# RWKV scan: the state scaled by the chunk's decay on ScalarE instead of GpSimd, under new order tables

## The chip, the cores and the metric

The kernel runs on one NeuronCore of a Trainium2 chip. The metric is the device time of one execution in microseconds; the median of several executions counts. TensorE is called PE here, VectorE DVE, ScalarE ACT and GpSimd POOL, as the profile does.

## What is computed

The reference is one inference step of a two-layer trunk with 640 tokens (512 latent, 128 context). Layer 0 mixes by attention and a gated linear recurrence, layer 1 by a bidirectional RWKV-7 scan, and each is followed by an MLP. The change touches the scan of layer 1 alone. Per head (16 heads of 64 channels) and per direction the reference runs

```
def step(s, inp):
    r_t, w_t, k_t, v_t, kk_t, a_t = inp
    sa = einsum('bhvk,bhk->bhv', s, -kk_t)
    s = s * w_t[:, :, None, :] + sa[..., None] * (kk_t * a_t)[:, :, None, :] + v_t[..., None] * k_t[:, :, None, :]
    return s, einsum('bhvk,bhk->bhv', s, r_t)
```

over the tokens, forwards and backwards. The kernel does it in chunks of 64 tokens: inside a chunk all is written as matrix products, and only the state `s`, 64x64 per head, passes from chunk to chunk. What comes out of a chunk is, by channel, decay times old state plus decay times the chunk's increment, where decay is the product of `w` over the chunk.

## The kernel before

The scan takes two heads at a time (a pair `q`, 0 to 7) and walks a pair in 5 tiles of 128 tokens, two chunks each, forwards and backwards at once. That gives 40 iterations `n`, and 5 of them make a pair. Below, turn 0 to turn 4 is the iteration with `n % 5` equal to 0 to 4.

Every engine has one queue of instructions that it runs strictly in order. What stands in it is laid out in Python: `run_iteration` goes through a table of names (`PE_ORDER`, `PE_FIRST`, `DVE_ORDER`, `ACT_FIRST`, `ACT_ORDER`, `POOL_ORDER`) and calls for each entry the task of that name, for iteration `n` plus the number beside the name. The engines meet by semaphores that each task waits on and raises. Nothing else sets the order. The tasks that matter here:

- **G, A1, A2, A3** prepare a chunk's inverse two or three iterations ahead: PE multiplies, DVE or ACT takes the product out of PSUM, POOL adds the identity (L2615 in `start`, L2622 in `plus_one`), and PE multiplies again.
- **GR, B1 to B5, BT** prepare the rest of the next iteration. For GR, DVE masks two 128x512 blocks (L2499).
- **x, u, s** are the walk itself, once for each of two chunks (x0, u0, s0, then x1, u1, s1; s1 stands in the next iteration). x: PE reads the state, DVE adds (L2520). u: PE multiplies that, ACT evacuates it (L2404). s: PE forms the increment, DVE writes the new state (L2531) from the increment and from `S2`, the old state times the decay.
- **S2** is made by POOL in its task x (`s2`, L2607): one 128x128 multiply of two state slices with a broadcast decay. It waits for the old state; DVE's `walk_s` waits for it.
- **y**: ACT evacuates the outputs of the iteration before (L2413). PE's x0 waits for it.
- **Once per pair**, for this pair or the next: the projections `prompt`, `w`, `a` with sigmoids on ACT (L2323, L2325), `cum0`, `cum1` (DVE scan L2446 and subtraction L2447), `keys0` to `keys3` (DVE, L2456 to L2470), `decays` (ACT), `staging` (DVE, four instructions L2476 to L2479 a tile), `k_sum`, `bonus_raw` (DVE, L2567 and L2568), `bonus`, `values`, `y_sum` (DVE L2552), `mean`, `var`, `y_norm` (L2560, L2561, L2564), `gate` (L2544), `final`, `state`.

DVE's entry for s, on which the change bears most, is in the code

```
dve.wait_ge(S("rwkv_s_psum"), k + 1)
dve.wait_ge(S("rwkv_s2"), k + 1)
```

and then one scalar_tensor_tensor for each direction.

Of the kernel before, what the change touches and what calls it, by code (L numbers as in the profile page):

```python
# [115 lines left out]
def program(nc, a, o):  # L116
    with ExitStack() as ctx:
# [1881 lines left out]
        def place(q, c):  # L1999
# [13 lines left out]
        DVE_ORDER = ("k_sum", "values", ("G", 2), "mean", "B5", ("s1", -1), ("keys2", -1), ("GR", 1), ("keys0", 1), "y_sum", "x0", "staging3", ("cum0", -1), "cum1",
                     "staging4", "staging1", "y_norm0", "keys3", "staging2", "s0", ("B3", 1), "staging0", ("bonus_raw", -1), "x1", "y_norm1", ("A3",
                     2), "keys1", ("B4", 1), ("gate", 1))
        ACT_FIRST = (("decays0", -1), ("decays3", 2), ("y1", -1), ("bonus", -1), ("mean", -1), ("a", -1), ("k_square", 2), ("state", 2), ("B1", 1), ("A1", 2), "decays1",
                     ("decays4", 2), "prompt", "u0", ("A2", 2), "var", ("final", -1), ("k_sum", 2), ("B2", 1), "w", ("BT", 1), "u1", ("decays2", 2))
# [284 lines left out]
        def rwkv_act(act, step):  # L2302
# [103 lines left out]

            def walk_y(n, s):
# [10 lines left out]
            tasks.update(dict(u=walk_u, y=walk_y, ahead=lambda m: out_ahead_act(act, m)))  # L2418
# [174 lines left out]
        def rwkv_pool(pool, step):  # L2593
# [428 lines left out]
```

## Time and profile before

| | us |
|---|---|
| median of three executions | 2197.14 (2193.59 to 2198.74) |
| the profiled execution | 2194.96 |
| its span, first to last instruction | 2193.2 |
| the scan within it | about 1187 to 1705 |
| a pair of the scan in the middle | 61.48 |

Of the page, the first part gives for each engine the busy time over the whole span: PE 93%, DVE 64%, ACT 47%, POOL 14%. This is an average over stages with different limits. Outside the scan PE multiplies large blocks nearly without a pause, and nothing there is touched. Inside the scan PE, DVE and ACT pass small blocks to one another. The profile is read there by turn: busy time of each engine in each of the five turns of one pair, then the pauses of PE and what ended them, then the single instructions around those pauses.

### The profile page before, as it was taken

Reading aid. Unit: us, or ns where it says so; the run is one execution under the profiler, and the core shown is the slowest. Engines: PE = TensorE matmul, PEld = TensorE weight load, DVE = VectorE, ACT = ScalarE, POOL = GpSimd, SP = SyncE. Lnnn points to the kernel's source line nnn. Section 1 sums busy time; section 2 is a strip of 40 time slices with the busy share of each in tenths; the row PEclk is TensorE's granted clock in tenths of the full one; section 3 lists DMA queues with packets and bytes.
Section 4 is the critical chain, followed back from the end, with each engine's and each line's share of the span. In section 5 each row is a group of like instructions: output and inputs, shape, how many; then the busy total and the mean of one; then the engine's idle time right before and its main releaser. Section 6 shows DMA issues by size and latency. Waiting matters only on the chain.

```text
span 2193.2 us, 60459 instructions
## 1 busy us (share of the span) xinstructions
PE 2041.7 (93%) x26203; PEld 1834.8 (84%) x26203; DVE 1408.8 (64%) x2698; ACT 1040.2 (47%) x1887; POOL 310.2 (14%) x542
## 2 busy tenths in 40 slices
PE   5999877898999999989998899999989999999999
PEld 3689754478999999967997777777777999999999
DVE  2242375655666666777644888888885478585757
ACT  5252354443535353567333666666664264434353
POOL 1000131001000000010001544444442200000000
PEclk8999999999999999999998999999999999999999
DMA  8212205960131313113210000000000211222312
GB/s 284 86 39 80 80 1 204 371 241 20 59 115 58 97 58 97 59 40 124 78 42 8 8 7 10 8 11 10 10 26 25 97 58 62 93 80 75 97 58 87
DMA packets 129764, 167.86 MB, mean 77 GB/s; under 512 B 13900, under 2 KB 87388, under 8 KB 129372
## 3 DMA queue, kind: packets, MB, share of 16 engines
q1 hardware_dynamic: 129500, 164.00, 22.3%
q8 instruction: 208, 3.41, 0.6%
q14 instruction: 56, 0.46, 0.1%
HBM read 160.44 MB, written 3.54 MB: 75 GB/s over the span
## 4 chain that ended last, share of the span: by engine, by line
PE 76%; DVE 9%; issue 7%; ACT 4%; POOL 2%; DMA 1%; PEld 1%; PEldq 0%; POOLq 0%; DVEq 0%; SPq 0%; ACTq 0%
PE psum L178 74%; ACT arena L1857 1%; DVE arena L2499 1%; ACT arena L1411 1%; DVE arena L2446 1%; PEld psum L178 1%; DMA arena<-in_x_prompt 1%; DVE small L1377 1%; PE psum L1342 0%; DVE arena L2470 0%; PE psum L2242 0%; POOL arena L2615 0%; ACT arena L642 0%; POOL arena L621 0%; DMA arena<-in_ada_w 0%
## 5 line engine op out<-in xcount | busy, mean ns | idle before, releaser
L178 PE MATMUL psum<-arena 64*64 64x64 f32 (+5 forms) x16064 | 575.2, 239 | 88.4 <-DVE arena L2520 16.4
L178 PEld LDWEIGHTS psum<-arena 64*64 64x64 f32 (+3 forms) x16064 | 460.2, 140 | 219.4 <-issue 102.7
L178 PE MATMUL psum<-hidden_high,weights_high 128*128 128x320 f32 x896 | 277.1, 309 | 0.5 <-DVE arena L1020 0.5
L178 PE MATMUL psum<-hidden_high,weights_low 128*128 128x320 f32 x896 | 276.9, 309 | 0.0
L178 PE MATMUL psum<-hidden_low,weights_high 128*128 128x320 f32 x896 | 276.9, 309 | 0.0
L178 PE MATMUL psum<-norm_low,weights_high 128*128 128x320 f32 x960 | 218.8, 309 | 0.0
L178 PE MATMUL psum<-norm_high,weights_low 128*128 128x320 f32 x960 | 218.7, 309 | 0.0
L178 PE MATMUL psum<-norm_high,weights_high 128*128 128x320 f32 x960 | 218.7, 309 | 0.0
L178 PEld LDWEIGHTS psum<-hidden_high,weights_high 128*128 128x128 f32 x896 | 168.2, 188 | 0.9 <-issue 0.7
L178 PEld LDWEIGHTS psum<-hidden_low,weights_high 128*128 128x128 f32 x896 | 168.2, 188 | 0.0
L178 PEld LDWEIGHTS psum<-hidden_high,weights_low 128*128 128x128 f32 x896 | 168.2, 188 | 0.0
L178 PEld LDWEIGHTS psum<-norm_high,weights_low 128*128 128x128 f32 x960 | 160.6, 188 | 0.0
L178 PEld LDWEIGHTS psum<-norm_high,weights_high 128*128 128x128 f32 x960 | 160.5, 188 | 0.0
L178 PEld LDWEIGHTS psum<-norm_low,weights_high 128*128 128x128 f32 x960 | 160.5, 188 | 0.0
L999 DVE TENSOR_TENSOR hidden<-hidden 128x640 f32<-128x640 f32 x32 | 26.4, 825 | 176.3 <-ACT hidden L946 176.3
L944 ACT ACTIVATE hidden<-psum 128x640 f32<-128x640 f32 x64 | 45.1, 705 | 189.7 <-PE psum L178 189.7
L899 ACT ACTIVATE weights_high<-weight_sums 128x512 fp32r<-128x512 f32 x128 | 76.8, 624 | 106.6 <-DVE weight_sums L918 55.6
L621 POOL TENSOR_TENSOR arena<-arena 128x640 f32<-128x640 f32 x24 | 41.7, 1738 | 569.8 <-ACT arena L613 569.1
L1020 DVE SCALAR_TENSOR_TENSOR arena<-psum,ada,arena 128x128 f32<-128x128 f32 (+2 forms) x208 | 83.4, 429 | 30.1 <-PE psum L178 29.2
L903 DVE TENSOR_TENSOR weights_low<-weight_sums,weights_high 128x512 fp32r<-128x512 f32 x128 | 88.1, 699 | 8.4 <-ACT weights_high L899 8.4
L899 ACT ACTIVATE weights_high<-weights 128x512 fp32r<-128x512 f32 x96 | 58.2, 622 | 68.3 <-PE psum L178 68.3
L2615 POOL TENSOR_TENSOR arena<-arena,constants 64x128 f32<-64x128 f32 x160 | 66.5, 415 | 157.3 <-DVE arena L2490 144.3
(268 smaller groups left out, 3986.7 us busy)
## 6 DMA issues: line engine op xcount, KB each, us to landing
weights<-in_mlp_w SPq DMA_DIRECT2D x64, 1024.0 KB, 5.3
arena<-in_ada_w SPq DMA_DIRECT2D x24, 2048.0 KB, 9.3
arena<-in_ab_w_in SPq DMA_DIRECT2D x6, 2048.0 KB, 7.8
arena<-in_ab_w_out SPq DMA_DIRECT2D x2, 2048.0 KB, 8.6
arena<-in_rwkv_wv SPq DMA_DIRECT2D x2, 2048.0 KB, 7.9
arena<-in_rwkv_wr SPq DMA_DIRECT2D x2, 2048.0 KB, 8.1
arena<-in_rwkv_wk SPq DMA_DIRECT2D x2, 2048.0 KB, 8.1
arena<-in_x_sample SPq DMA_DIRECT2D x1, 2048.0 KB, 10.0
```

The source lines that it names most:

```text
L178: return nc.tensor.matmul(out, lhsT, rhs, start=start, stop=stop, skip_group_check=shared)
L621: G.tensor_tensor(total, a0 if k == 1 else total, (a0, a1)[k % 2], ALU.add).then_inc(S("norm_squares_added"), 1)
L899: A.activation(slots_of(WHI)[:, j], slot_raw(l, grp, i, j), ACT.Copy).then_inc(S("slot_high"), 1)
L903: V.tensor_tensor(slots_of(WLO)[:, j], slot_raw(l, grp, i, j), slots_of(WHI)[:, j], ALU.subtract)\
L944: A.activation(h, PS[:, 2 * j:2 * j + 2, 0:HN], ACT.Relu).then_inc(S("up_evacuated"), 1)
L999: V.tensor_tensor(h[:, H_T1:H_T3 + 1, :], h[:, H_B11:H_B22 + 1:3, :], h[:, H_B12:H_B12 + 1, :].broadcast_to([P, 2, HN]), ALU.subtract)\
L1020: ins = V.scalar_tensor_tensor(x, PS[:, bank, c:c + t1 - t0], gate[:, m, g:g + 1], x, ALU.mult, ALU.add)
L1377: step(V.tensor_reduce(st[:, 0:1], pair(2 * h, k), AXX, ALU.max))
L1411: A.activation(PR[m % 2][:, h, 0:k], pair(2 * h, k), ACT.Exp, scale=ATTN_SCALE, bias=st[:, 1:2], accum_out=st[:, 2:3]).then_inc(S("att_exp ...
L1857: A.activation(XI[s % 2][:, k, :], unit(U_H, 8)[:, k, :], ACT.Identity, scale=OMM[:, 8 * mrow + k:8 * mrow + k + 1])\
L2446: step(V.tensor_tensor_scan(y, m, x, 0.0, ALU.mult, ALU.add))
L2615: ins = G.tensor_tensor(P1[HALF[h], d, 0], QD[r, h, 0], units(r), ALU.add)
```

## The change

POOL's task for S2 goes. ACT gets a task `decayed_state` under the name x: two ACTIVATE copies of 128x64, one for each direction, from the state to `S2`, each with the decay column as its per-partition scale. It waits for the same two semaphores, and raises the same one, which DVE's `walk_s` still waits on. All order tables are written anew. PE's, DVE's and POOL's work is otherwise the same, instruction for instruction.

```
+            def decayed_state(n, s):
+                (cs, us), k = steps_of(n, s), 2 * n + s
+                act.wait_ge(S("rwkv_state"), k)
+                act.wait_ge(S("rwkv_state_in"), n // 5 + 1)
+                for d in range(2):
+                    ins = A.activation(S2[:, d, :], ST[d][:, cs[d], :], ACT.Copy, scale=PE_[:, (n // 5) % 2, d, cs[d]:cs[d] + 1])
+                ins.then_inc(S("rwkv_s2"), 1)
...
-            def s2(n, s):
-                (cs, us), k = steps_of(n, s), 2 * n + s
-                pool.wait_ge(S("rwkv_state"), k)
-                pool.wait_ge(S("rwkv_state_in"), n // 5 + 1)
...
-                G.tensor_tensor(S2, st, dec.broadcast_to([P, 2, 64]), ALU.mult).then_inc(S("rwkv_s2"), 1)
-                pool.wait_ge(S("rwkv_s2"), 2 * n + s + 1)
...
-        POOL_ORDER = ("G", ("B0", -1), ("x0", -2), "A1", "A2", ("x1", -2))
+        POOL_ORDER = (("A2", -2), ("G", -1), ("B0", -2), ("A1", -1))
```

What the tables move, as it stands in the queues, turn by turn:

| turn | before | after |
|---|---|---|
| 0, DVE | GR, keys0, y_sum, x0 | GR, y_sum, x0 |
| 0, PE | GR, B1, A1, prompt, x0, u0, B2, A2, w | GR, A1, x0, B1, prompt, u0, A2, B2, w |
| 0 to 4, ACT | y1, (decays), B1, A1, ... u1 | y1, S2 of x0, A1, B1, (decays), ... S2 of x1, u1 |
| 1 to 4, PE | GR, B1, x0, A1, ... u0 | GR, A1, B1, x0, ... u0 |
| 1, DVE | x0, cum0, cum1, s0, B3, x1, A3, keys1, B4 | x0, keys0, cum0, cum1, s0, B3, keys1, x1, A3, B4 |
| 1 and 2, PE | var of the pair before stands behind the G that ends turn 1 | var stands before u1 of turn 1 |
| 2, DVE | B5, s1, keys2, GR, x0, y_norm0, keys3 | B5, y_norm0, s1, GR, x0, keys2, keys3 |
| 2 and 3, PE | gate, u1, G, B5, final, s1 | final, u1, gate, G, B5, s1 |
| 3 and 4, DVE | bonus_raw before x1 of turn 4 | bonus_raw before x1 of turn 3 |

On DVE, turn 1 of pair 3 (iteration 16), before: the new state of turn 0 (L2531), the masks of GR (L2499), x0 (L2520), the two cumulations, s0 and what follows.

```order
L2531 SCALAR_TENSOR_TENSOR arena<-psum,arena 128x64 [waits rwkv_s2,rwkv_s_psum]
...
L2499 TENSOR_TENSOR arena<-psum,constants 128x512 [waits rwkv_s_psum,b_product]
...
L2520 TENSOR_TENSOR arena<-psum,arena 128x128 [waits b_scalar,rwkv_x_psum]
L2446 SCALAR_TENSOR_TENSOR arena<-constants,arena 128x640 [waits rwkv_sig]
L2447 TENSOR_TENSOR arena<-arena 128x640 [waits vector_step]
L2446 SCALAR_TENSOR_TENSOR arena<-constants,arena 128x640 [waits rwkv_sig]
L2447 TENSOR_TENSOR arena<-arena 128x640 [waits vector_step]
L2531 SCALAR_TENSOR_TENSOR arena<-psum,arena 128x64 [waits rwkv_s2,rwkv_s_psum]
...
L2510 TENSOR_TENSOR arena<-psum,arena 128x256 [waits b_product]
L2520 TENSOR_TENSOR arena<-psum,arena 128x128 [waits b_scalar,rwkv_x_psum]
L2505 TENSOR_TENSOR arena<-psum,constants 128x256 [waits a_product]
```

The same place of the changed kernel, whose line numbers are 9 higher here:

```order
L2540 SCALAR_TENSOR_TENSOR arena<-psum,arena 128x64 [waits rwkv_s2,rwkv_s_psum]
...
L2508 TENSOR_TENSOR arena<-psum,constants 128x512 [waits rwkv_s_psum,b_product]
...
L2529 TENSOR_TENSOR arena<-psum,arena 128x128 [waits b_scalar,rwkv_x_psum]
L2465 TENSOR_SCALAR small<-param_cols 128x1
L2469 SCALAR_TENSOR_TENSOR arena<-arena,param_cols 128x640 [waits rwkv_staged,rwkv_k_rs,vector_step]
L2455 SCALAR_TENSOR_TENSOR arena<-constants,arena 128x640 [waits rwkv_sig,vector_step]
L2456 TENSOR_TENSOR arena<-arena 128x640 [waits vector_step]
L2455 SCALAR_TENSOR_TENSOR arena<-constants,arena 128x640 [waits rwkv_sig]
L2456 TENSOR_TENSOR arena<-arena 128x640 [waits vector_step]
L2540 SCALAR_TENSOR_TENSOR arena<-psum,arena 128x64 [waits rwkv_s2,rwkv_s_psum]
```

The two instructions of keys0 (L2465, L2469) now stand between x0 and the cumulations, so ahead of s0.

On ACT, turn 0 of pair 3 (iteration 15), before: y1 (L2413), B1 (L2384), A1 (L2376), the table load and the sigmoids of `prompt`, and u0 (L2404).

```order
L2413 ACTIVATE arena<-psum 128x128 [waits rwkv_ysum,rwkv_state]
...
L2384 ACTIVATE arena<-psum 128x512 [waits b_product]
L2376 ACTIVATE arena<-psum 128x512 [waits a_product]
L2323 ACT_TABLE_LOAD [waits rwkv_lora,rwkv_staged]
L2323 ACTIVATE arena<-psum,param_cols 128x128 [waits rwkv_bonus_raw]
...
L2404 ACTIVATE arena<-psum 64x128 [waits rwkv_u_psum]
...
L2380 ACTIVATE arena<-psum 128x768 [waits a_product]
```

And in the changed kernel, where y1 is L2422, A1 L2377, B1 L2385, u0 L2405 and the copies of S2 are L2413:

```order
L2422 ACTIVATE arena<-psum 128x128 [waits rwkv_ysum,rwkv_state]
...
L2413 ACTIVATE arena<-arena 128x64 [waits rwkv_state_in,rwkv_state]
L2413 ACTIVATE arena<-arena 128x64
L2377 ACTIVATE arena<-psum 128x512 [waits a_product]
L2385 ACTIVATE arena<-psum 128x512 [waits b_product]
L2324 ACT_TABLE_LOAD [waits rwkv_lora,rwkv_staged]
L2324 ACTIVATE arena<-psum,param_cols 128x128 [waits rwkv_bonus_raw]
...
L2405 ACTIVATE arena<-psum 64x128 [waits rwkv_u_psum]
```

The two copies came in ahead of A1 and B1, and A1 and B1 changed places; the table load, the sigmoids and u0 stand as they did.

## Rows read from the trace of the kernel before

**Rows 1.** Page, part 1: busy time, share of the span, instructions.
```profile
PE 2041.7 (93%) x26203; PEld 1834.8 (84%) x26203; DVE 1408.8 (64%) x2698; ACT 1040.2 (47%) x1887; POOL 310.2 (14%) x542
```
**Rows 2.** Windows, turns 0 to 4: length, busy us of PE, PEld, DVE, ACT, POOL; clock.
```profile
1386.03:1399.57 13.54, 11.79 (x407) 9.78 (x400) 8.42 (x21) 9.63 (x22) 5.82 (x12) 1.00 0.01 4
1399.57:1412.18 12.61, 11.55 (x379) 9.34 (x375) 11.58 (x22) 8.78 (x20) 5.84 (x12) 1.00 0.02 6
1412.18:1424.85 12.67, 10.86 (x366) 9.28 (x366) 12.30 (x27) 7.20 (x17) 5.81 (x12) 1.00 0.01 3
1424.85:1436.24 11.39, 11.25 (x396) 9.83 (x390) 10.07 (x25) 6.06 (x16) 5.20 (x12) 1.00 0.08 17
1436.24:1447.51 11.27, 11.00 (x386) 9.56 (x380) 10.23 (x27) 7.56 (x23) 5.51 (x12) 1.00 0.09 22
```
**Rows 3.** Waits of PE in 1285 to 1592 (five pairs): total us, times, longest.
```profile
PE psum L178 <- DVE arena L2520: 9.6, 10, 1.4
PE psum L178 <- DVE arena L2531: 5.4, 10, 0.7
```
**Rows 4.** Timeline, DVE, turn 0: start us, us, engine, line, [idle before <-releaser].
```profile
1388.46 1.29 DVE L2499 TENSOR_TENSOR arena<-psum,constants 128x512 f32<-128x512 f32 x2 [0.36 <-PE psum L178]
...
1389.85 0.94 DVE L2460 SCALAR_TENSOR_TENSOR arena<-arena,param_cols 128x640 f32<-128x640 f32 x1
...
1391.68 0.29 DVE L2520 TENSOR_TENSOR arena<-psum,arena 128x128 f32<-128x128 f32 x1
```
**Rows 5.** Timeline, PE, turn 0.
```profile
1392.02 4.62 PE L178 MATMUL psum<-arena 64*64 64x64 f32 x176 [1.44 <-DVE arena L2520]
...
1393.64 1.09 PE L178 MATMUL psum<-arena 64*64 64x512 f32 x8
```
**Rows 6.** Timeline, ACT, turn 0.
```profile
1390.61 1.28 ACT L2323 ACT_TABLE_LOAD   x1 [0.42 <-PE psum L178]
1391.90 1.14 ACT L2323 ACTIVATE arena<-psum,param_cols 128x128 f32<-128x128 f32 x4
1392.91 0.55 ACT L2404 ACTIVATE arena<-psum 64x128 f32<-64x128 f32 x2
```
**Rows 7.** Timeline, DVE, turn 1.
```profile
1401.99 1.29 DVE L2499 TENSOR_TENSOR arena<-psum,constants 128x512 f32<-128x512 f32 x2 [0.61 <-PE psum L178]
1403.19 0.28 DVE L2520 TENSOR_TENSOR arena<-psum,arena 128x128 f32<-128x128 f32 x1
...
1408.17 0.47 DVE L2531 SCALAR_TENSOR_TENSOR arena<-psum,arena 128x64 f32<-128x64 f32 x2
```
**Rows 8.** Timeline, PE, turn 1.
```profile
1408.69 2.47 PE L178 MATMUL psum<-arena 64*64 64x64 f32 x104 [0.61 <-DVE arena L2531]
```
**Rows 9.** Timeline, DVE, end of turn 2 and turn 3.
```profile
1423.81 0.41 DVE L2506 COPY arena<-psum 128x256 f32<-128x256 f32 x1
...
1427.54 1.29 DVE L2499 TENSOR_TENSOR arena<-psum,constants 128x512 f32<-128x512 f32 x2 [0.61 <-PE psum L178]
```
**Rows 10.** Timeline, PE, end of turn 2 and turn 3.
```profile
1424.37 1.16 PE L178 MATMUL psum<-arena 64*64 64x64 f32 x48 [0.47 <-DVE arena L2506]
1425.34 0.45 PE L178 MATMUL psum<-constants,arena 64*64 64x64 f32 x8
```
**Rows 11.** Lines in 1285 to 1592: xcount, busy us, mean ns, idle before.
```profile
L2371 ACT ACTIVATE arena<-arena 128x256 f32<-128x256 f32 x25 | 10.2, 410 | 0.0
...
L2335 ACT ACTIVATE arena<-psum 128x64 f32<-128x64 f32 x10 | 1.7, 222 | 0.1
```
**Rows 12.** Lines in 1285 to 1592, DVE and POOL.
```profile
L2479 DVE TENSOR_TENSOR arena<-arena 128x256 f32<-128x256 f32 x25 | 14.7, 589 | 0.0
...
L2568 DVE SCALAR_TENSOR_TENSOR arena<-arena,param_cols 128x640 f32<-128x640 f32 x5 | 4.5, 907 | 0.2
...
L2607 POOL TENSOR_TENSOR arena<-arena 128x128 f32<-128x128 f32 x50 | 25.4, 508 | 6.3 <-POOL arena L2622 2.5
```
**Rows 13.** Timeline, POOL, around the cumulations of turn 1.
```profile
1402.91 0.40 POOL L2607 TENSOR_TENSOR arena<-arena 128x128 f32<-128x128 f32 x1
```

More of the change, by code:

```diff
@@ L2001, in place @@
             return c if c < 8 else c + 2 * (q % 2)
-        PE_ORDER = ("prompt", "mean", "var", "B5", ("final", -1), ("s1", -1), ("GR", 1), ("B1", 1), "x0", ("A1", 2), "a", "w", "state", "bonus", "u0", ("B2", 1), ("A2",
-                     2), "s0", ("B3", 1), ("BT", 1), "x1", ("A3", 2), ("B4", 1), ("values", 1), ("k_sum", 1), ("gate", 1), "u1", ("G", 3))
+        PE_ORDER = ("mean", "B5", ("s1", -1), ("GR", 1), ("A1", 2), ("B1", 1), "x0", "state", "a", "bonus", "u0", ("B2", 1), ("A2", 2), "s0", ("B3", 1), "prompt", ("BT",
+                     1), "x1", "w", ("A3", 2), ("B4", 1), ("var", 1), ("values", 1), "final", ("k_sum", 1), "u1", ("gate", 1), ("G", 3))
         def with_ahead(order, after):
@@ L2013, in program @@
[L2013 to L2017, printed above, removed]
+        PE_FIRST = ("B5", ("bonus", 1), ("s1", -1), ("GR", 1), ("A1", 2), "x0", ("B1", 1), "prompt", "u0", ("A2", 2), ("B2", 1), ("mean", -1), "w", ("state", 1), "s0",
+                     ("k_sum", 2), ("A3", 2), ("final", 1), ("B3", 1), "x1", ("a", -1), ("BT", 1), ("B4", 1), "u1", ("G", 3), ("var", -1), ("gate",
+                     2), ("values", 2))
@@ new lines, in program @@
+        DVE_ORDER = ("values", "k_sum", "gate", ("G", 2), "mean", "B5", "y_norm0", ("s1", -1), ("GR", 1), "y_sum", "x0", "staging3", "keys0", "staging1", "staging4",
+                     "staging2", ("cum0", -1), ("keys2", -1), "cum1", "keys3", "s0", ("B3", 1), "bonus_raw", "y_norm1", "keys1", "x1", "staging0",
+                     ("A3", 2), ("B4", 1))
+        ACT_FIRST = (("k_sum", 2), ("decays2", 2), ("decays0", -1), "decays1", ("decays4", 2), ("y1", -1), "x0", ("A1", 2), ("B1", 1), "prompt", ("k_square", 2), ("mean",
+                     -1), "u0", ("A2", 2), ("state", 2), ("B2", 1), ("a", -1), ("bonus", -1), "w", ("BT", 1), "x1", "var", ("decays3", 2), ("final",
+                     1), "u1")
@@ L2019, in first_of_pair @@
         def first_of_pair(n):
             return n >= 0 and n % 5 == 0 and n + 5 < NB
-        ACT_ORDER = (("y1", -1), "decays2", "decays3", ("B1", 1), ("A1", 2), "a", "decays4", "bonus", "u0", "state", ("B2", 1), ("A2", 2), "mean", ("decays1", 1),
-                     ("k_square", 1), ("BT", 1), "prompt", ("decays0", 1), "u1", ("k_sum", 1), "final", "w", ("var", 1))
-        POOL_ORDER = ("G", ("B0", -1), ("x0", -2), "A1", "A2", ("x1", -2))
+        ACT_ORDER = ("decays3", "decays0", "mean", ("y1", -1), "x0", ("A1", 2), ("B1", 1), ("decays1", 1), "decays2", "decays4", "state", "a", "bonus", "u0", ("B2", 1),
+                     ("A2", 2), "w", ("k_square", 1), ("BT", 1), "final", "x1", ("var", 1), "u1", ("k_sum", 1), "prompt")
@@ L2652, in rwkv_pool @@
             tasks = dict(G=start, A1=squares, A2=fourths, B0=values)
-            tasks.update(dict(x=s2))
             for n in range(-4, NB + 2):
```

9 lines of the change are left out of this document (1 added, 8 removed).

## The prediction

> **What bounds the kernel now.** The page comes first: PE is busy 93% of the span [rows 1], but most of that is large products outside the scan, which the change leaves alone. So I read the scan, and there one pair by its five turns [rows 2]. They take 13.54 + 12.61 + 12.67 + 11.39 + 11.27 = 61.48 us. PE is busy 56.45 us of it, DVE 52.60, ACT 39.23, POOL 28.18. The reader is to see two things. PE is nearly full in turns 3 and 4 (11.25 of 11.39, 11.00 of 11.27), and DVE is nearly full in turn 2 (12.30 of 12.67). And the slack lies in turns 0 to 2, where PE stands still for 1.75, 1.06 and 1.81 us. That is 5.03 us a pair with the 0.4 of turns 3 and 4, and no reordering can win more. The granted clock is 1.00 in all five, so the clock plays no part.
>
> The pauses of PE that have a name are waits for DVE's x (L2520, 9.6 us in five pairs) and for the new state (L2531, 5.4 us) [rows 3]. POOL's multiply, which the change removes, is not among them. The chain through the pauses is always the same: PE has run ahead, and DVE still has something in its queue before the entry that PE wants.
>
> **S2 leaves POOL.** Ten multiplies a pair of 508 ns [rows 12] are 5.1 us of POOL's 28.2. POOL is busy under half of a pair, so on the path this is worth nothing directly. What it can free is DVE, which slows down beside POOL: the last instruction of a staging (L2479) takes 589 ns on average [rows 12], where an instruction of DVE on 256 columns alone takes 0.41 us (L2506, [rows 9]). That is 0.18 us for each of five stagings, 0.9 us a pair, most of it in turns 3 and 4, where DVE is not the bound, and some of it beside POOL work that stays. I take 0.2 us a pair over all of DVE's work where it is the bound, and keep 0 and 0.6.
>
> The Trainium skill (SBUF, on the shared port pair) says that a GpSimd instruction and a DVE instruction with two SBUF inputs exclude each other for the whole instruction. By that, DVE would be held off for up to the length of each multiply. What it would give as a result is a rival below.
>
> **S2 comes to ACT.** Two copies of 128x64, ten times a pair. The same shape from PSUM without a scale column takes 222 ns, and ten of them, in twos, are 1.7 us busy; a larger one from SBUF takes 410 ns for 128x256 [rows 11]. So two of them take between 0.34 and 0.82 us, and I take 0.5, nearer to the row of the same shape. ACT gets 5 us a pair more and is then busy 44 of 61.5. The S2 of x1 stands before u1, for which ACT waits anyway. The S2 of x0 stands behind y1 and ahead of A1 and B1. Behind it in ACT's queue are A1, B1 and later u0; A1's evacuation is wanted by POOL and then by the end of A2 on PE, B1's by B2. PE now runs A1 ahead of B1 and x0, so that its product is ready for ACT sooner by what these take, more than the 0.5 of the copies. In turn 2, where y1 comes late, B1 should come out of ACT about when PE reaches B2; I put 0.1 us on this, inside the sum of turns 2 and 3. I cost the S2 of x0 at nothing elsewhere. If that cover were gone it would cost up to 0.5 us in each turn.
>
> **A1 before x0 on PE, turns 1 to 4.** PE's u0 wants DVE's x0, which stands behind the two masks of GR, 1.29 us [rows 7]. While they run PE has the same A1, B1 and x0 to do in either order. The order costs nothing as long as the masks set the time.
>
> **Turn 0: keys0 leaves, and B1 and prompt go between x0 and u0.** Before, DVE runs masks, keys0 (to 1390.79), y_sum, and only then x0, done at 1391.97 [rows 4]; PE starts u0 at 1392.02 after 1.44 us of standing still [rows 5]. Without keys0 x0 is done 1.1 us earlier, about 1390.8. But ACT is next: the table load can't start before PE's prompt is done (1390.61), and load, sigmoids and u0's evacuation run to 1393.46 [rows 6] whether u0 is early or not. PE's w has to wait until the sigmoids of prompt have read its banks, 1391.90 + 1.14 = 1393.04. In the trace PE starts w at 1393.64 [rows 5], so w can move forward by some 0.55 us, no more. s0 and all behind it follow w. **Gain 0.55**, between 0.3 (A3 finds POOL late) and 1.1.
>
> **Turn 1: keys0 arrives.** Between DVE's x0 (done at 1403.47) and the new state (begun at 1408.17) there are only the cumulations, 4.7 us, and PE waits 0.61 us for that state [rows 7, 8]. With keys0 between, which was the time from the masks' end at 1389.75 to 1390.79 [rows 4], this is later by 1.1 us, and PE is already waiting. **Cost 1.1**, between 0.9 and 1.2. Here DVE is the bound and stays it up to the gate of turn 2: B3, keys1, A3, the G masks, y_norm0, keys2 and keys3, staging0. The tables permute these, and DVE runs them without a pause before and after, so their order neither gains nor costs. var before u1 makes the evacuation of u1 on ACT late by about 1 us; DVE has y_norm0 ahead of s1 in that time, which covers it.
>
> **Turns 2 and 3: final moves.** Before, PE gets out of DVE's hold at 1424.37 (G, 0.47 us after it was ready, behind DVE's A3 [rows 9, 10]) and has G, B5, final (0.45 [rows 10]), s1 and GR to do until the masks at 1427.54, for which DVE waits 0.61 us [rows 9]. After, final is done while PE waits for DVE's A3 anyway, with gate behind it. The masks can begin earlier by final and about 0.2 of that pause, at most by the 0.61 that DVE waits. **Gain 0.6**, between 0.3 and 0.6.
>
> **Turns 3 and 4: bonus_raw moves forward by a turn.** Its second instruction takes 0.91 us [rows 12] and its first about as much, both in front of DVE's x1. In turn 3 DVE is idle 11.39 - 10.07 = 1.3 us and in turn 4 1.0 us [rows 2], so of 1.8 us put into turn 3 up to 0.5 stick out, and PE, which was idle for 0.14 us there, follows: **cost 0.3**, between 0 and 0.6. Turn 4 is relieved: **gain 0.15** of PE's 0.27 us of pause.
>
> **The sum.** -0.55 + 1.1 - 0.6 + 0.3 - 0.15 = +0.1, and -0.2 for DVE without the multiplies: -0.1 us a pair. Turns of this kind come seven times (keys0 and cumulations for pairs 1 to 7), so -0.7 us; the first and the last turns of the scan have neither keys nor sigmoids in new places and I put them at 0. The profiled execution of 2194.96 us, 1.8 of it outside its span of 2193.2, becomes 2194.3. The median of the three runs is 2.2 above it, so 2196.4.
>
> **Rivals.** Forecast: as summed, within 0.2% (4.4 us), which is about what a measurement of this kernel can tell from no change. The cases:
>
> 1. Slower, 2202. The 1.1 us of keys0 is the mechanism. It decides if DVE, from x0 of turn 1 to the masks of turn 3, gives nothing back: then final's place saves nothing (PE would then wait for DVE's masks and not DVE for PE), DVE's relief is 0, and +1.1 - 0.55 + 0.3 - 0.15 = +0.7 a pair, times 7 is +4.9; with bonus_raw at its upper bound +7. For it: DVE is busy 12.30 of 12.67 in turn 2. Against: DVE does wait 0.61 us before the masks of turn 3 [rows 9]. 0.26.
> 2. Faster, 2189. The pause before u0 (1.44) goes by 1.1 and not by 0.55, because w finds room elsewhere in PE's queue, and DVE gains 0.6 instead of 0.2: -0.1 - 0.55 - 0.4 = -1.05 a pair, -7.4. For it: 1.44 is the longest pause of the pair. Against: the sigmoid chain on ACT, which has no slack in the rows. 0.20.
> 3. Faster, 2184. POOL's multiplies hold DVE off for their whole length, and their absence sets it free where it is the bound: four multiplies in turns 1 and 2 of 0.40 us are -1.6 a pair, -1.7 with the sum, -12. Against it: a multiply at 1402.91 lies inside the masks of turn 1 [rows 13], and these take 1.29 us there as in turn 0, where no multiply does [rows 4, 7]. By that rule of the Trainium skill (SBUF) only instructions with two SBUF inputs would be held, and the masks read PSUM, so the trace doesn't contradict it. 0.12.
> 4. Slower, 2214. The S2 of x0 is exposed on ACT in each turn: 0.5 x 5 = 2.5 us a pair over 7 pairs, +17.5. For it: ACT is in the walk's chain by u. Against: it is idle 22 us of the pair [rows 2], and 0.42 us right before the table load [rows 6]. 0.04.
>
> **How the numbers follow.** The forecast has 0.38. Same by more than 0.2% in neither direction: 0.38. Faster: 0.20 + 0.12 = 0.32. Slower: 0.26 + 0.04 = 0.30. The range takes in cases 1 to 3 with the bounds of the unknown costs: low ends 0.3 + 0.5 for turn 0 and DVE's relief give -12 over seven pairs, high ends (bonus_raw 0.6, final 0.3, turn 0 0.3, keys0 1.2) give +1.1 a pair, +8, and some exposed S2 on top. I give 2184 to 2208.
>
> **What would show it.** Right: in a middle pair of the changed kernel PE waits for x (L2529) well under 1.44 us in turn 0 and 1.5 to 1.9 us for the state (L2540) in turn 1; the pair takes 61 to 62 us; DVE's idle time before the masks of turn 3 stays at some 0.6 us or less; ACT is busy about 44.5 us a pair. Wrong: a pause of PE before B2 or the end of A2 that ACT ends (case 4), cumulations and key steps on DVE that got visibly shorter (case 3), or a turn 1 that doesn't grow by a microsecond. What would upset the sum is a wait that the trace of before doesn't show at all, since every turn of this scan is held by three queues at once.

## The result, and the profile after it

The changed kernel takes 2204.89 us (median of 6 runs, 2203.32 to 2209.69), the kernel before 2197.15 us (6 runs, 2191.82 to 2198.74): ratio 1.0039, 95% interval 1.0027 to 1.0051. It is slower by 7.7 us. The time lies in the range of 2184 to 2208, but the forecast, no difference that can be measured, was wrong: the change costs. The profiled executions are 2194.96 us before and 2204.85 us after, with spans of 2193.2 and 2203.1 us.

Page of the changed kernel, part 1, against [rows 1]:

```profile
PE 2054.6 (93%) x26203; PEld 1844.0 (84%) x26203; DVE 1405.8 (64%) x2698; ACT 1075.9 (49%) x2047; POOL 265.6 (12%) x462
```

S2 has moved as the change says: POOL has 80 instructions and 45 us less, ACT 160 instructions and 36 us more. But PE is busy 13 us longer for the same 26203 products. Busy time alone doesn't say why: part of it comes at an unchanged clock (57.28 us in a middle pair without a stretch at half clock, 56.45 before). So the granted clock has to be read beside it.

The windows of the changed kernel, against [rows 2]. The first five rows are the turns of the pair that starts at 1329.25, the sixth is turn 1 of the next pair, the last a stretch inside that turn. Columns: length, busy us of PE, PEld, DVE, ACT, POOL with counts, granted clock, DMA share, GB/s.

```profile
1329.25:1342.29 13.04, 12.13 (x403) 9.82 (x396) 7.09 (x19) 10.92 (x27) 4.64 (x10) 1.00 0.03 6
1342.29:1356.00 13.71, 11.42 (x379) 9.47 (x376) 12.57 (x23) 9.07 (x20) 4.53 (x10) 1.00 0.01 2
1356.00:1368.74 12.74, 11.49 (x388) 9.76 (x380) 12.23 (x27) 8.90 (x27) 4.97 (x10) 1.00 0.03 7
1368.74:1380.28 11.54, 11.32 (x388) 9.73 (x381) 10.88 (x27) 6.98 (x20) 4.22 (x10) 1.00 0.05 13
1380.28:1391.46 11.18, 10.91 (x392) 9.58 (x385) 9.41 (x25) 8.03 (x25) 4.24 (x10) 1.00 0.09 22
1404.50:1419.71 15.21, 12.93 (x379) 10.43 (x377) 12.56 (x23) 9.29 (x20) 4.53 (x10) 0.89 0.01 4
1415.90:1419.30 3.40, 3.40 (x45) 2.33 (x44) 2.00 (x6) 1.59 (x2) 0.00 (x0) 0.51 0.00 0
```

The reader is to compare the second row with the sixth. It is the same turn with the same 379 products and the same work of DVE, once 13.71 us at a granted clock of 1.00, once 15.21 us at 0.89. In the second case PE spends 3.4 us at half clock (1.2 of 2.4 GHz), where only 45 products are run, and the turn is 1.50 us longer.

Such stretches of 3.4 us begin in the changed kernel at 1228.1, 1289.6, 1415.9 and 1542.1, always in turn 1 of a pair, in pairs 0, 1, 3 and 5. From the first B5 of the scan on, the seven pairs of the kernel before have none. First the four stretches, then those seven pairs before:

```profile
1228.10:1231.50 3.40, 3.12 (x86) 2.94 (x78) 2.34 (x6) 0.81 (x3) 0.00 (x0) 0.50 0.03 5
1289.60:1293.00 3.40, 3.40 (x49) 2.31 (x42) 2.40 (x6) 1.31 (x2) 0.00 (x0) 0.50 0.00 0
1415.90:1419.30 3.40, 3.40 (x45) 2.33 (x44) 2.00 (x6) 1.59 (x2) 0.00 (x0) 0.51 0.00 0
1542.10:1545.50 3.40, 3.40 (x57) 2.39 (x54) 1.72 (x5) 1.89 (x3) 0.00 (x0) 0.51 0.00 0
```
```profile
1203.70:1634.70 431.00, 391.91 (x13191) 333.44 (x13181) 367.05 (x816) 275.99 (x670) 199.13 (x420) 1.00 0.04 9
```

This is no accident of the profiled executions. The mean granted clock of the whole span is 0.978 to 0.981 in all six executions of the changed kernel, and 0.980 to 0.987, on average 0.984, in the 83 executions of the kernel before that ran beside the experiments. Four stretches of 3.4 us at half clock take 0.003 off the mean.

From the first B5 to the B5 seven pairs later the pairs take, in us:

| pair | 0 | 1 | 2 | 3 | 4 | 5 | 6 | sum |
|---|---|---|---|---|---|---|---|---|
| before | 59.33 | 61.48 | 61.48 | 61.48 | 61.79 | 62.56 | 62.79 | 430.92 |
| after | 60.58 | 63.70 | 62.21 | 63.71 | 62.21 | 64.16 | 63.02 | 439.59 |

The difference is 8.67 us. (The spans differ by 9.9. The other 1.2 us arise ahead of pair 0, 0.9 of it in code that the change leaves alone, and nothing is added behind the seven pairs.) Four stretches at 1.50 us are 6.0 of it, and 2.7 is the order itself: +0.73 in pair 2 (62.21 against 61.48), which would be 2.2 for pairs 1 to 3, and smaller amounts in the others. The 1.50 is measured in pairs 1, 3 and 5, where turn 1 takes 15.2 us and not 13.7; in pair 0 it is taken over from them.

PE's waits in 1285 to 1592 after the change (total us, times, longest), against [rows 3]:

```profile
PE psum L178 <- DVE arena L2540: 9.8, 5, 2.0
PE psum L178 <- ACT arena L2405: 4.4, 14, 0.7
PE psum L178 <- DVE arena L2529: 3.8, 10, 0.4
PE psum L178 <- ACT arena L2324: 2.1, 5, 0.6
```

The long waits have changed their kind. Before, there were ten for x with 9.6 us, at most 1.4. Now five waits for the new state make 9.8 us, 2.0 each: one a pair, in turn 1. This is the place in the pair from 1391.46, first on PE and then on DVE:

```profile
1414.96 1.51 PE L178 MATMUL psum<-arena 64*64 64x64 f32 x56 [1.95 <-DVE arena L2540]
1416.22 2.38 PE L178 MATMUL psum<-arena,constants 64*64 64x320 f32 x8
```
```profile
1408.26 0.29 DVE L2529 TENSOR_TENSOR arena<-psum,arena 128x128 f32<-128x128 f32 x1
1408.65 0.97 DVE L2469 SCALAR_TENSOR_TENSOR arena<-arena,param_cols 128x640 f32<-128x640 f32 x1
1409.66 1.49 DVE L2455 TENSOR_TENSOR_SCAN arena<-constants,arena 128x640 f32<-128x640 f32 x1
...
1414.44 0.46 DVE L2540 SCALAR_TENSOR_TENSOR arena<-psum,arena 128x64 f32<-128x64 f32 x2
```

keys0 (L2469) stands between x0 and the cumulations, and the state comes at 1414.44, 6.2 us after x0 instead of 5.0 [rows 7]. PE stands still for 1.95 us. Then x1, A3 and B4 (56 instructions) take 1.51 us and `var` (64x320, eight instructions) 2.38. In the pair before the pause is 1.96 us, the clock stays at 1.00, and the same instructions behind it take the usual 1.28 and 1.26:

```profile
1352.76 1.28 PE L178 MATMUL psum<-arena 64*64 64x64 f32 x56 [1.96 <-DVE arena L2540]
1353.86 1.26 PE L178 MATMUL psum<-arena,constants 64*64 64x320 f32 x8
```

### The profile page after: what moved, and what is told of

It is laid out like the page before. It is cut to its first block, busy times and chain, and to the rows that moved or that the text cites. A ratio compares the mean times of both kernels' runs of the same rounds, so it can differ in the third digit from the quotient of the medians.

```text
span 2203.1 us, 60533 instructions
## 1 busy us (share of the span) xinstructions
PE 2054.6 (93%) x26203; PEld 1844.0 (84%) x26203; DVE 1405.8 (64%) x2698; ACT 1075.9 (49%) x2047; POOL 265.6 (12%) x462
## 4 chain that ended last, share of the span: by engine, by line
PE 78%; ACT 7%; issue 7%; DVE 6%; DMA 1%; POOL 1%; PEld 1%; PEldq 0%; POOLq 0%; DVEq 0%; ACTq 0%; SPq 0%
PE psum L178 76%; ACT arena L1857 1%; ACT arena L1411 1%; DVE arena L2508 1%; PE psum L2243 1%; PEld psum L178 1%; DVE small L1377 1%; DMA arena<-in_x_prompt 0%; PE psum L1342 0%; ACT arena L642 0%; DMA arena<-in_ada_w 0%; POOL arena L1754 0%; DVE arena L1385 0%; ACT L2324 0%; ACT arena L2405 0%
## 5 line engine op out<-in xcount | busy, mean ns | idle before, releaser
L178 PE MATMUL psum<-arena 64*64 64x64 f32 (+5 forms) x16064 | 584.9, 240 | 87.8 <-ACT arena L1411 14.8
L178 PEld LDWEIGHTS psum<-arena 64*64 64x64 f32 (+3 forms) x16064 | 467.4, 141 | 221.3 <-issue 96.6
```

The costliest lines, as they stand in the source:

```text
L178: return nc.tensor.matmul(out, lhsT, rhs, start=start, stop=stop, skip_group_check=shared)
```

## The experiments

Three theories stood against each other. **T1, order and clock:** keys0 in turn 1 makes the pause, the pause costs 1.1 us by itself, and 1.5 more wherever a stretch at half clock follows. **T2, order alone:** the stretches only come along, and the time is lost in DVE's and ACT's queues. **T3, S2 on ACT:** the copies delay what ACT owes to PE. All ratios are against the kernel before, run on the same chip beside them. The rows come from four chips, so where two rows are compared with each other, their ratios count more than their times.

| run | us | before | ratio (95%) | half-clock stretches | first seven pairs, us |
|---|---|---|---|---|---|
| s2_alone | 2196.96 | 2198.05 | 0.9996 (0.9986 to 1.0007) | 1 | 432.58 |
| tables_alone | 2209.92 | 2198.05 | 1.0049 (1.0037 to 1.0062) | 6 | 448.17 |
| keys0_turn0 | 2192.57 | 2198.05 | 0.9976 (0.9968 to 0.9985) | 0 | 428.69 |
| filled_pause | 2205.29 | 2198.05 | 1.0037 (1.0021 to 1.0052) | 0 | 441.19 |
| filled_wide | 2201.48 | 2197.47 | 1.0020 (1.0011 to 1.0029) | 0 | 437.21 |
| keys0_moved_alone | 2208.43 | 2197.47 | 1.0049 (1.0037 to 1.0062) | 4 | 442.39 |
| cum1_late | 2206.88 | 2197.47 | 1.0044 (1.0032 to 1.0057) | 5 | 443.66 |
| bonus_turn4 | 2189.90 | 2197.47 | 0.9966 (0.9955 to 0.9977) | 0 | 428.91 |
| keys0_turn0_pool | 2196.84 | 2196.76 | 1.0003 (0.9992 to 1.0014) | 1 | 433.39 |
| keys0_behind_x0 | 2192.75 | 2196.76 | 0.9983 (0.9973 to 0.9992) | 0 | 430.02 |
| y_norm0_behind | 2202.73 | 2196.76 | 1.0028 (1.0017 to 1.0038) | 4 | 439.71 |
| var_behind | 2200.48 | 2198.26 | 1.0013 (1.0003 to 1.0023) | 1 | 439.92 |

**s2_alone: the old tables, S2 on ACT.** `decayed_state` with x0 behind y1 and x1 before u1 on ACT, all other order as before.

> The kernel before with its own order tables; only S2 moved from GpSimd to ScalarE (copies for x0 right behind y1, for x1 right ahead of u1). Theory P (the pause of turn 1: keys0 ahead of the cumulations costs 1.1 us a pair and lets the clock fall): no long pause is made here, so about 2197 (2193 to 2200), pair 61.3 to 61.6, clock 1.00 through the scan. Rival S (the two copies on ScalarE, 0.58 us each time, hold up the evacuations): 2201 to 2205, with waits of PE for ScalarE grown.

No difference that can be measured, and one stretch at half clock, in turn 0 of pair 5, where none was expected. So T3 falls: the copies are not what costs.

**tables_alone: the new tables, S2 on POOL.** `decayed_state` out, `s2` back on POOL at its old place:

```
-        ACT_ORDER = ("decays3", "decays0", "mean", ("y1", -1), "x0", ("A1", 2), ...
+        ACT_ORDER = ("decays3", "decays0", "mean", ("y1", -1), ("A1", 2), ...
-        POOL_ORDER = (("A2", -2), ("G", -1), ("B0", -2), ("A1", -1))
+        POOL_ORDER = ("G", ("B0", -1), ("x0", -2), "A1", "A2", ("x1", -2))
```

> The new order tables of PE, DVE and ScalarE with S2 still on GpSimd, in GpSimd's old order. Theory P: like the changed kernel, 2203 to 2207, pause of PE before x1 of turn 1 about 1.9 us, pair 62.2, or 63.7 with a stretch at half clock. Rival S: 2195 to 2199, since ScalarE does no S2.

The tables alone cost 11 to 12 us (by the ratio and by the medians), with six stretches and an undisturbed turn 1 of 13.9 us. So the loss is in the tables. By its first seven pairs, 448.17 us against 439.59, S2 on ACT would even give something back under the new tables, though some 3 us of that are the two stretches more; the intervals of the two ratios overlap, so this run doesn't settle it.

**keys0_turn0: the changed kernel with keys0 back in turn 0**, though behind x0, not in front of it:

```
-... ("GR", 1), "y_sum", "x0", "staging3", "keys0", "staging1", ...
+... ("GR", 1), "y_sum", "x0", ("keys0", 1), "staging3", "staging1", ...
```

> The changed kernel with keys0 taken from turn 1 back to turn 0, but behind DVE's x0, where DVE stood idle for 3.4 us in the kernel before. Theory P: turn 1 shrinks from 13.7 to 12.6 us, turn 0 stays at 13.0, no stretch at half clock inside the pairs, pair 61.1: 2205 - 7 x 1.1 - 4 x 1.5 = 2191 (2188 to 2195). Rival S: not below 2199. Rival O (the other moved entries, var, bonus_raw, A1 before x0, are what costs): 2197 to 2200.

2192.57 us: 12.3 us less than the changed kernel (14 by the ratios), 5.5 less than before, no stretch at half clock. Turn 0 keeps its gain (13.05 us) and turn 1 falls to 12.59, where the kernel before had 12.61. The waits of PE in the same five pairs as above:

```profile
PE psum L178 <- ACT arena L2405: 5.0, 15, 0.5
PE psum L178 <- DVE arena L2540: 4.2, 5, 0.8
```

One entry of DVE's table makes the whole loss. What it does not tell is how much of that is the pause and how much the clock, since both go together.

**filled_pause and filled_wide: the pause filled.** The changed kernel with products whose result nobody reads, in front of x1 of turn 1. They stand right where the pause was, and the semaphore that they wait for is raised before it. A pair gets eight products of 128 columns in the first kernel (16 instructions) and two of 448 in the second (four instructions):

```
+                if s == 1 and n % 5 == 1 and n < 35:
+                    pe.wait_ge(S("a_scalar"), 2 * (n + 2) + A_SC["Q4"])
+                    for _ in range(2):
+                        mm(PS[:, 0, 64:512], ident, CON[:, 0:448])
```

> The changed kernel with 8 extra 128x128 products with 128 columns, whose result nobody reads, on PE in the pause before x1 of turn 1; they wait only for an evacuation that is long done by then. If the four stretches at clock 0.5 follow from PE standing still, they go, every middle pair takes 62.2 us, and the time is 2205 - 6 = 2199 (2197 to 2201). If the stretches come from elsewhere they stay and the time is 2204 to 2207. If the products stick out of the pause, turn 1 grows.

The stretches are gone, and the time is not: 2205.29 us. For T1 that looked like a refutation. But turn 1 itself takes 13.7 us in each of the pairs 1 to 6, as the undisturbed one of the changed kernel does. The time is lost in other turns: in pair 2, turn 3 takes 13.30 us and not 11.54. The waits of PE between 1200 and 1680 show what stands there; here "issue" stands for time in which PE waits for nothing that the profile shows. First filled_pause, then the changed kernel:

```profile
PE psum L178 <- issue: 12.6, 23, 1.6
```
```profile
PE psum L178 <- issue: 3.4, 11, 0.7
```

This kernel has 9.2 us more of such waits, in 23 places and not 11, over half of them in the first three pairs. None of the other kernels here has more than 6.3 us of them. So the filling most likely spoilt its own test, and I made it out of fewer and wider products.

> The changed kernel with the pause before x1 of turn 1 filled by 2 wide products (128x128 by 448 columns, result unread) instead of the 8 narrow ones, which removed every stretch at half clock but cost 9 us of TensorE's own issue waits. With 4 instructions a pair instead of 16 the issue waits should stay near the 3.4 us of the changed kernel. If the stretches at half clock cost 1.5 us each, this gives 2205 - 6 = 2199 (2197 to 2202), clock 1.00 through the scan, all middle pairs 62.2. If the stretches are not what makes the difference between 62.2 and 63.7: 2204 to 2206.

The place in filled_wide. The 1.95 us of pause are 0.26, and what stands behind them runs at full clock:

```profile
1412.31 1.77 PE L178 MATMUL psum<-constants 128*128 128x448 f32 x4
1414.33 1.28 PE L178 MATMUL psum<-arena 64*64 64x64 f32 x56 [0.26 <-DVE arena L2544]
```

The pair is 62.20 us, against 62.21 undisturbed and 63.71 with a stretch in the changed kernel (first row filled_wide, then the changed kernel):

```profile
1390.83:1453.03 62.20, 59.04 (x1905) 49.06 (x1898) 52.16 (x118) 43.90 (x117) 22.66 (x50) 1.00 0.04 10
```
```profile
1391.46:1455.17 63.71, 58.87 (x1901) 49.27 (x1894) 52.19 (x118) 43.91 (x117) 22.58 (x50) 0.97 0.04 10
```

PE still doesn't get the state any earlier, but the pair costs 1.51 us less. Turn 1 takes 13.69 to 13.78 us in pairs 1 to 6; in the changed kernel it takes 13.7 in three of them and 15.2 in the other three:

```profile
1278.23:1292.01 13.78, 13.25 (x383) 10.22 (x381) 12.51 (x23) 9.07 (x20) 4.54 (x10) 1.00 0.01 4
1403.87:1417.57 13.70, 13.11 (x383) 10.15 (x380) 12.56 (x23) 9.07 (x20) 4.52 (x10) 1.00 0.02 4
1528.27:1541.96 13.69, 13.11 (x382) 10.14 (x380) 12.55 (x23) 9.06 (x20) 4.52 (x10) 1.00 0.01 4
```

The ratio is 1.0020 where the changed kernel has 1.0039; the intervals overlap only at their ends. The difference is 4 us of the 6 that the stretches should be worth. The rest is not accounted for: pairs 1 and 2 take 62.9 and 62.8 us, and the waits for issue, 5.9 us here, are no more than other kernels have without a filling. T2 falls in this form: part of the loss is the clock. The rest, 1.0020, is the order with what the filling itself costs.

**keys0_moved_alone: the kernel before with keys0 alone moved** from turn 0 to behind x0 in turn 1.

```
-... ("GR", 1), ("keys0", 1), "y_sum", "x0", "staging3", ("cum0", -1), ...
+... ("GR", 1), "y_sum", "x0", "keys0", "staging3", ("cum0", -1), ...
```

> The kernel before with one entry moved: DVE's keys0 from turn 0 (ahead of x0) to turn 1 (between x0 and the cumulations), S2 on GpSimd. Theory P: the pause before x1 of turn 1 grows from 0.61 to 1.7 us, turn 1 from 12.6 to 13.7, turn 0 shrinks by up to 0.5 but no more (ScalarE's sigmoids hold w): +0.6 x 7 = +4, and with the stretches at half clock +1.5 each, up to +14: 2201 to 2212. Rival O (the other moves of the tables matter more): 2197 to 2199.

The old tables with this one entry give the pause, the stretches and the time, 1.0049. The turn 1 from 1338.61, without a stretch, takes 14.03 us, with one up to 15.3:

```profile
1349.15 2.48 PE L178 MATMUL psum<-arena 64*64 64x64 f32 x104 [2.04 <-DVE arena L2531]
```

**cum1_late: another way out**, with keys0 in turn 0 and, beside it, cum1 and keys1 moved to the end of turn 1, behind A3 and B4.

> Made from the kernel with keys0 back in turn 0 behind x0 (2192.6): cum1 of turn 1 moved from ahead of s0 to behind A3, and keys1 to behind B4. If the pause of 0.8 us before x1 of turn 1 is DVE's queue alone, it goes, and turn 1 falls from 12.6 to about 11.8: 2192.6 - 7 x 0.8 = 2187. If DVE's work is the bound over turns 1 and 2 as a whole, the pause comes back in turn 2 (before s1 or x0) and the time stays at 2192 to 2193.

A miss. Turn 1 falls only to 12.84, and turn 2 grows to 14.0 without and 14.9 with a stretch. At its start PE waits twice:

```profile
1353.05 3.56 PE L178 MATMUL psum<-arena 64*64 64x64 f32 x112 [0.99 <-DVE arena L2519]
1358.34 0.34 PE L178 MATMUL psum<-arena 64*64 64x64 f32 x8 [1.73 <-ACT arena L2422]
```

cum1 now stands in front of B4, and keys1 in front of B5 and y_norm0 of turn 2. They delay B5, and over the new state that DVE makes behind them also y1 on ACT, for which PE waits next. The 2.4 us of a cumulation cost no less at the end of turn 1 than in front of the state. The run also shows that the stretches are no matter of turn 1 or of keys0: they went to the place where the pause now is.

**bonus_turn4: keys0_turn0, and bonus_raw back before x1 of turn 4** (`"bonus_raw"` becomes `("bonus_raw", -1)`).

> Made from the kernel with keys0 back in turn 0 (2192.6): bonus_raw back from turn 3 to turn 4, where it stood in the kernel before. By the term of the prediction (cost 0.3 in turn 3, gain 0.15 in turn 4) turn 3 falls from 11.54 to about 11.2 and turn 4 grows from 11.18 to 11.3: 2192.6 - 1 = 2191.5. If bonus_raw's place is worth nothing: 2192.6.

Turn 3 is 11.13 us instead of 11.54, turn 4 between 11.41 and 12.05 instead of 11.18. So the entry costs 0.41 us where it is put, and about as much comes back where it is taken away; the first seven pairs take 428.91 us, as in keys0_turn0. At 0.9966 it is the fastest kernel of this study, faster than both, but its interval overlaps that of keys0_turn0, so I claim nothing for this entry.

**keys0_turn0_pool: keys0_turn0 with S2 back on POOL.**

> The new tables with keys0 in turn 0 behind x0 (which gave 2192.6 with S2 on ScalarE), but S2 on GpSimd again. It measures what moving S2 is worth where no stretch at half clock confuses the comparison. By the prediction's term (DVE relieved by 0.2 us a pair, bounds 0 and 0.6): 2192.6 + 1.4, up to + 4.2. By the two kernels with the new tables (turn 1 13.71 against 13.88, turn 2 12.74 against 12.92, pauses counted): 2192.6 + 7 x 0.36 = 2195. If the long pauses of the kernel with the tables alone are needed for its loss: 2192.6.

No different from the kernel before, and 4.3 us slower than keys0_turn0 (5.9 by the ratios), with ratios that lie apart. Under the new tables S2 on ACT is worth something that it isn't under the old ones. In the profiled executions the first seven pairs differ by 4.7 us, of which 2.0 are in pair 0, with its stretch, and 2.7 in pairs 1 to 6. One wait that goes with it, in turn 0, is for POOL. In 1285 to 1592, first here, then in keys0_turn0:

```profile
PE psum L178 <- POOL arena L2623: 3.6, 5, 0.8
```
```profile
PE psum L178 <- POOL arena L2620: 1.6, 5, 0.3
```

The line is POOL's step of A, for which PE waits within A2. In turn 0 the new order of PE has A2 ahead of B2 and so asks for it earlier, and on POOL the multiply of S2 (L2608) stands in front of it; PE waits 0.81 us in the turn from 1323.72, and 0.33 in the same turn of keys0_turn0:

```profile
1328.73 0.98 POOL L2608 TENSOR_TENSOR arena<-arena 128x128 f32<-128x128 f32 x1
1329.79 0.64 POOL L2623 TENSOR_TENSOR arena<-arena,constants 128x256 f32<-128x256 f32 x1
```

The other part is DVE's. In pair 2, turn 0 takes 13.30 us against 13.05 in keys0_turn0, turn 1 12.83 against 12.59 and turn 2 12.94 against 12.75, and in turns 1 and 2 DVE is busy longer by about that, 11.76 against 11.52 and 12.42 against 12.24. The place in turn 1 is keys1, two instructions on DVE with two inputs from SBUF. With a multiply of S2 beside them they take 1.76 us, and in keys0_turn0 1.55:

```profile
1346.54 0.40 POOL L2608 TENSOR_TENSOR arena<-arena 128x128 f32<-128x128 f32 x1
```
```profile
1346.60 1.76 DVE L2465 SCALAR_TENSOR_TENSOR arena<-arena 128x640 f32<-128x640 f32 x2
```
```profile
1346.30 1.55 DVE L2473 SCALAR_TENSOR_TENSOR arena<-arena 128x640 f32<-128x640 f32 x2
```

In this kernel a stretch at half clock also follows a wait for POOL, in pair 0:

```profile
1220.71 2.53 PE L178 MATMUL psum<-arena 64*64 64x64 f32 x44 [1.60 <-POOL arena L2623]
```

**keys0_behind_x0: the kernel before with keys0 moved behind x0**, still in turn 0.

```
-... ("GR", 1), ("keys0", 1), "y_sum", "x0", "staging3", ...
+... ("GR", 1), "y_sum", "x0", ("keys0", 1), "staging3", ...
```

> The kernel before with one entry moved: DVE's keys0 in turn 0 from ahead of y_sum and x0 to behind x0. The pause of PE before u0 (1.44 us) should shrink to about 0.4. By the prediction's reading w is held by ScalarE's sigmoids, so turn 0 falls by 0.5 only, from 13.54 to 13.05: 2197.3 - 3.5 = 2193.8. If ScalarE doesn't hold it, turn 0 falls by 1.1 and the time is 2189.6.

As expected. Turn 0 is 13.08 us in place of 13.54, and the pause of 1.44 us before u0 [rows 5] is 0.47:

```profile
1330.85 5.12 PE L178 MATMUL psum<-arena 64*64 64x64 f32 x176 [0.47 <-DVE arena L2520]
```

All that the change wins in turn 0 comes from keys0 not standing before x0. For that it needn't leave the turn.

**y_norm0_behind: bonus_turn4 with y_norm0 behind x0 of turn 2**, to take away DVE's delay of the masks of GR there.

> Made from the fastest kernel so far (keys0 in turn 0, bonus_raw in turn 4, 2189.9): y_norm0 of turn 2 moved from ahead of s1 to behind x0. PE's pauses of 0.34 to 0.40 us before s1, x0 and u0 of turn 2 should go. If DVE's queue is the bound to the end of turn 2, the time is given back at G there (wait for L2515), and it stays at 2189 to 2190. If not, up to 0.7 us in each of 7 pairs: 2185.

A miss. Turn 2 takes 14.28 us without and up to 15.60 with a stretch. y_norm0 now stands with keys2 and keys3 between x0 and the state, which is later by it, and PE has one long pause there:

```profile
1359.42 1.40 PE L178 MATMUL psum<-arena 64*64 64x64 f32 x56 [2.12 <-DVE arena L2540]
```

**var_behind: bonus_turn4 with var back behind G** on PE, and behind u1 on ACT, so that DVE's masks of G at the start of turn 2, which wait 0.57 us for PE, come sooner.

```
-        PE_ORDER = ("mean", "B5", ...  ("B4", 1), ("var", 1), ("values", 1), "final", ...
+        PE_ORDER = ("mean", "var", "B5", ...  ("B4", 1), ("values", 1), "final", ...
```

> Made from the fastest kernel so far (2189.9): var back behind the G that ends turn 1 on PE, and behind u1 on ScalarE, as in the kernel before. DVE waited 0.57 us for that G at the start of turn 2, which the prediction left out when it called DVE's queue free of pauses there. If that wait is what turns 1 and 2 lost, they shrink together by up to 0.5 us a pair: 2186.5 to 2188. If PE then waits for var's evacuation before GR, as it did by 0.42 us in the kernel before, and DVE's y_norm0 for the same, it is given back: 2190 or more.

A miss too: turns 1 and 2 take 13.67 and 13.09 us in place of 12.58 and 12.74. `var` was what PE ran while DVE did keys1 ahead of x1; without it PE waits for x1 (L2529), and G is not earlier. The row is from pair 5, where a stretch at half clock follows; the wait is 0.72 us in the other pairs too.

```profile
1538.68 1.88 PE L178 MATMUL psum<-arena 64*64 64x64 f32 x48 [0.72 <-DVE arena L2529]
```

## Why the prediction was wrong

**Turn 0, gain 0.55: right.** 13.54 to 13.04, so 0.50. The limit was where the prediction put it: before w PE waits 0.38 us for the sigmoids of ACT (L2324 in the waits above, 2.1 us in five pairs), and before u0 only 0.39 for x.

**Turn 1, cost 1.1: right.** 12.61 to 13.71 undisturbed. The pause is 1.95 us, a little over the 1.5 to 1.9 that were named.

**"DVE runs them without a pause before and after": wrong.** DVE waits 0.57 us at the start of turn 2:

```profile
1356.27 0.69 DVE L2499 TENSOR_TENSOR arena<-psum,constants 128x512 f32<-128x512 f32 x1 [0.57 <-PE psum L178]
```

In the kernel before these masks of G start without a wait. The late state is not the reason: keys0_turn0, where the state comes in time, has the same wait of 0.57 us there. It comes with the other entries, since now x1 stands behind keys1 on DVE, and var (1.26 us) stands ahead of u1 and G on PE. Turn 2 takes 12.74 us instead of 12.67, although DVE has no more to do in it. var_behind shows that the place of var alone is not to blame: without it there the turns are longer.

**Final's move, gain 0.6: mis-sized.** Turn 2 gains nothing (+0.07). Turn 3 without bonus_raw (bonus_turn4) takes 11.13 us where it took 11.39, so 0.26 is what is left of it. **bonus_raw, cost 0.3 and gain 0.15:** 0.41 in turn 3 (11.54 against 11.13); turn 4 goes from 11.27 to 11.18. Turns 2 to 4 together give +0.07 + 0.15 - 0.09 = +0.13, where the sum had -0.6 + 0.3 - 0.15 = -0.45.

**S2 off POOL, relief of DVE 0.2: right in size, not in what becomes of it.** DVE is busy 52.17 us in the pair in place of 52.60, 0.43 less. The staging lines fell from 589, 494, 456 and 450 ns to these, in the same window as [rows 12]:

```profile
L2487 DVE TENSOR_TENSOR arena<-arena 128x256 f32<-128x256 f32 x25 | 14.8, 591 | 0.0
L2486 DVE TENSOR_TENSOR arena<-arena 128x256 f32<-128x256 f32 x25 | 11.3, 454 | 0.0
L2485 DVE TENSOR_TENSOR arena<-arena 128x256 f32<-128x256 f32 x25 | 10.3, 414 | 0.0
L2488 DVE TENSOR_TENSOR arena<-arena 128x256 f32<-128x256 f32 x25 | 10.3, 413 | 0.0
```

A line of 591 ns is still there without any multiply on POOL, now the third and not the last, so the 589 of [rows 12] were not the multiply's doing alone. The four fall from 49.6 to 46.7 us in five pairs, 0.6 us a pair; with S2 alone moved (s2_alone) their mean times sum to 1879 ns instead of 1989. Most of the stagings lie in turns 3 and 4, where DVE is not the bound. Where it is, the relief does shorten a turn: turn 2 of s2_alone takes 12.41 us instead of 12.67, with DVE busy 12.04 instead of 12.30. Turn 4 gives it back (11.61 to 12.21 us in pairs 1 to 5, 11.27 to 11.91 before), for a reason that no run here shows. Rival 3, DVE held off for the length of each multiply and 12 us won, falls: s2_alone takes just the multiplies away and is at 0.9996. The Trainium skill (SBUF — State Buffer, section "SBUF: two separate sides") makes the shared pair of ports an exclusive lock between a GpSimd instruction that reads SBUF and a DVE instruction with two SBUF inputs or in a two-port mode, not between all instructions. The trace agrees with that in kind, since the stagings got faster and the masks from PSUM (L2508, 685 ns on average, 686 before) did not, and since keys1 took 0.21 us longer beside a multiply of 0.40. How much of the ten multiplies lay beside such work was not counted, so the length of the lock stays untested.

**S2 on ACT: 0.5 us for two, off the path: right within its bounds.** 345 ns each, 0.59 for two:

```profile
L2413 ACT ACTIVATE arena<-arena 128x64 f32<-128x64 f32 x96 | 28.0, 345 | 6.5 <-DVE arena L2540 6.5
```

ACT is busy 43.91 us a pair, 44 was named. PE waits 4.4 us for u (L2405) in five pairs, where it was 1.1 before; tables_alone, without the copies, has 3.5 of it, so most of that is the order. Rival 4 falls. What the prediction didn't see is the gain on the other side: with the new order of PE, POOL's step of A would have been late (3.6 us of waits in five pairs of keys0_turn0_pool, 1.6 in keys0_turn0). With the relief of DVE in turns 1 and 2 (0.43 us in pair 2) moving S2 was worth 4.3 us there.

**The sum.** A pair at full clock got +0.73 us. That is the +0.7 of rival 1, and in the main for its reason: keys0's 1.1 us were not given back, and final's place saved nothing in turn 2. Over the scan it makes 2.7 us and not 4.9, because pairs 0 and 4 to 6 lose less than the middle one (pair 4 +0.42, pair 6 +0.23, pair 0 without its stretch -0.25). That rival 1 named 2202 and 2204.89 was measured is in part luck: its mechanism made 2.7 us, and the clock, which it left out, made more.

**"The clock plays no part": the step that failed most.** Four stretches at half clock cost 6.0 of the 8.67 us. The prediction read the granted clock of before, 1.00 in all five turns, and took it for a property of the stage. It is one of the schedule: the pause of PE before the state, which the sum itself made 1.1 us longer (0.6 to about 1.7), was priced at what PE loses in it, and what PE runs behind it was priced at full clock. The rows held nothing of that price, as no pause of the middle pairs was longer than 1.44 us and none was followed by a stretch. A case for it, with a bound taken from the start of the scan (13.7 us at half clock end at 1196.5 in the kernel before), was missing from the rivals.

**What stays open.** Why pairs 1, 3 and 5 have the stretch and 2 and 4 don't, with pauses of 1.96 and 1.95 us before the same work. The split of 6.0 and 2.7 is read from one execution, and the share of pair 0 is an estimate: turn 1 of pair 0 takes 14.85 us with its stretch and 13.93 in both filled kernels, which would make it 0.9 and not 1.5. filled_wide supports the split with 4 us. What delays PE in filled_pause isn't settled either, only that it is booked under issue.

## What to carry to other kernels

When an edit lengthens a pause of TensorE in a stage that is otherwise full, price the pause twice: for what it lasts, and for the chance that the products behind it run at half clock. A step of VectorE that nobody waits for soon goes right behind the entry that TensorE wants, within the same turn, and not into a turn where the vector queue is already the bound. A unit of work that is moved between engines is worth what the new order asks of the old engine: test it under both orders, since here it was worth nothing under one and some 4 to 6 us under the other.

## What the runs showed of the hardware

- **Pauses and the clock.** Stretches of 3.4 us at a granted clock of 0.5 came behind pauses of PE of 1.95 us in some pairs and not in others. In the changed kernel each cost 1.5 us against the same turn without one; in cum1_late it was 0.9 (14.89 against 13.99) and in y_norm0_behind 1.3 (15.60 against 14.28). The kernels with one pause of 1.7 us or more in each middle pair (the changed one, tables_alone, keys0_moved_alone, cum1_late, y_norm0_behind) have four to six stretches; those whose longest there is under 1.5 us have none or one. Of the 30 such pauses in pairs 1 to 6 of those five kernels, 20 were followed by a stretch. Among the others, one stretch stands behind a wait of 1.38 us, in s2_alone, one behind 1.60 us in pair 0, in keys0_turn0_pool, and one behind 0.84 and 0.72 us close together, in var_behind, so a short pause is no safeguard.
- **Many small extra products may have a price outside their place.** With 16 instructions more in each pair the waits for issue in 1200 to 1680 were 12.6 us. In the other thirteen kernels, the one with four wide ones (5.9) among them, they were 1.9 to 6.3. It is one profiled execution.
- **DVE beside POOL.** Ten multiplies of 508 ns less on POOL made the stagings 0.6 us a pair shorter (0.55 in s2_alone). One multiply of 0.40 us beside keys1 made that 0.21 us longer. The masks that read PSUM kept their 685 ns.
